# Second attention of a two-block kernel: products of split operands, remainders on GpSimd, out-projection by halves of k

## The reference

```python
def attn_mixer(h_ctx, h_lat, qkv_w, q_norm_w, k_norm_w, out_w, cos, sin, ctx_out):
    def project(u):                              # qkv_w: 1024 x 1536
        q, k, v = jnp.split(u @ qkv_w, [D_ATTN, D_ATTN + N_KV_HEADS * HEAD_DIM], axis=-1)
        q = rmsnorm(q.reshape(b, L, N_KV_HEADS, Q_PER_KV, HEAD_DIM), q_norm_w)
        k = rmsnorm(k.reshape(b, L, N_KV_HEADS, HEAD_DIM), k_norm_w)
        return q, k, v.reshape(b, L, N_KV_HEADS, HEAD_DIM)
    ...                                          # rope on q and k of the tokens
    s = jnp.einsum('bqkgd,bskd->bkgqs', q_blk, k) * scale      # keys: tokens and context
    p = jax.nn.softmax(s, axis=-1)
    o = jnp.einsum('bkgqs,bskd->bqkgd', p, v)
    out_lat = o.reshape(b, S, D_ATTN) @ out_w    # out_w: 1024 x 1024
# around it, in layer 1:
h_lat = rmsnorm(x, norm1_w[i]) * (1.0 + sc1l) + sh1l           # and h_ctx from ctx
x = x + g1l * o_lat
x = x + g2l * moe_ec(rmsnorm(x, norm2_w[i]) * (1.0 + sc2l) + sh2l, ...)
```

## Time and profile before

| | |
|---|---|
| median of three runs | 2139.0 us |
| profiled execution | 2138.3 us, its span 2136.4 us |
| TensorE matmul, busy share of the span | 93% |
| DVE, ACT, POOL, busy share | 44%, 31%, 5% |
| HBM read | 620.8 MB, 291 GB/s over the span |
| mean granted clock of TensorE | 0.984 |

### The profile page before, as it was taken

How to read it: one execution, slowest core, us unless ns; L and a number is a source line. 1 busy time by engine, 2 the same in 40 slices (tenths; PEclk the granted TensorE clock), 3 DMA queues, 4 the chain that set the end, 5 groups by cost and what they waited for, 6 DMA issues and landing times.

```text
span 2136.4 us, 24699 instructions
## 1 busy us (share of the span) xinstructions
PE 1988.2 (93%) x10028; PEld 1075.2 (50%) x10028; DVE 934.0 (44%) x1680; ACT 666.9 (31%) x1304; POOL 96.3 (5%) x105
## 2 busy tenths in 40 slices
PE   9988988999899999999899999988999899999887
PEld 6845644444578888878533333322444433333222
DVE  5667425454887888853612222221665301111101
ACT  5254313111577776752311110100244111111001
POOL 0101000000101000100000000000210000000000
PEclk9989989999999999999999999999999999999999
DMA  9637878998043334325599999999820699999997
GB/s 370 217 123 276 288 286 324 383 404 327 25 141 119 106 112 154 105 77 216 212 422 429 427 427 428 427 427 424 332 97 1 269 416 426 427 427 427 427 426 324
DMA packets 143376, 623.58 MB, mean 292 GB/s; under 512 B 10976, under 2 KB 61280, under 8 KB 105376
## 3 DMA queue, kind: packets, MB, share of 16 engines
q1 hardware_dynamic: 141104, 618.83, 72.7%
q10 hardware_dynamic: 2160, 3.18, 0.4%
HBM read 620.80 MB, written 1.18 MB: 291 GB/s over the span
## 4 chain that ended last, share of the span: by engine, by line
PE 73%; DMA 14%; DVE 7%; ACT 3%; issue 2%; SPq 1%; POOL 1%; DVEq 0%; POOLq 0%; ACTq 0%
PE bank L3216 21%; DMA slots<-in_moe_w 10%; PE bank L564 7%; PE bank L566 7%; PE bank L565 7%; PE bank L634 6%; PE bank L1972 4%; PE bank L3237 2%; DMA spare_slot<-in_moe_w 2%; PE bank L1999 2%; DMA hT<-in_moe_w 2%; PE bank L3187 2%; PE bank L2514 1%; PE bank L1102 1%; PE bank L1956 1%
## 5 line engine op out<-in xcount | busy, mean ns | idle before, releaser
L3216 PE MATMUL bank<-slots,xgTe 128*64 128x512 f32 (+1 forms) x1392 | 312.2, 594 | 28.5 <-DMA slots<-in_moe_w 28.5
L3486 DVE TENSOR_TENSOR actse<-sge,bank 32x512 f32<-32x512 f32 (+1 forms) x48 | 32.8, 683 | 501.9 <-PE bank L3216 273.5
L3216 PEld LDWEIGHTS bank<-slots,xgTe 128*64 128x64 f32 (+1 forms) x1392 | 93.5, 125 | 228.4 <-issue 193.8
L3379 ACT ACTIVATE sge<-bank 32x512 f32<-32x512 f32 (+1 forms) x48 | 28.4, 591 | 463.4 <-PE bank L3216 463.2
L3216 PE MATMUL bank<-slots,aTe 128*64 128x512 f32 (+1 forms) x688 | 156.9, 601 | 13.7 <-issue 12.5
L565 PE MATMUL bank<-slots_r 128*128 128x512 f32 x416 | 163.4, 393 | 0.0
L564 PE MATMUL bank<-hT_r,slots_r 128*128 128x512 f32 x384 | 155.6, 405 | 0.0
L566 PE MATMUL bank<-slots_r 128*128 128x512 f32 x384 | 152.0, 396 | 0.0
L3391 ACT ACTIVATE aTe<-bank 128x512 f32<-128x512 f32 x32 | 19.1, 597 | 282.9 <-PE bank L3290 282.9
L2419 DVE TENSOR_TENSOR slots_r<-slots,slots_r 128x2048 fp32r<-128x2048 f32 x32 | 76.7, 2396 | 68.2 <-ACT slots_r L2414 68.1
L3216 PEld LDWEIGHTS bank<-slots,aTe 128*64 128x64 f32 (+1 forms) x688 | 49.8, 126 | 105.6 <-issue 102.9
(11 more groups left out here) (615 smaller groups left out, 3320.8 us busy)
## 6 DMA issues: line engine op xcount, KB each, us to landing
slots<-in_moe_w SPq DMA_DIRECT2D x127, 2048.0 KB, 26.8
spare_slot<-in_moe_w SPq DMA_DIRECT2D x22, 2048.0 KB, 25.8
slots<-in_ada_w SPq DMA_DIRECT2D x20, 2048.0 KB, 10.9
extra0e<-in_moe_w SPq DMA_DIRECT2D x20, 2048.0 KB, 28.3
slots<-in_ssd_in_w SPq DMA_DIRECT2D x48, 512.0 KB, 5.3
slots<-in_moe_w_gate SPq DMA_DIRECT2D x20, 1024.0 KB, 9.0
slots<-in_moe_w_up SPq DMA_DIRECT2D x20, 1024.0 KB, 11.2
slots<-in_moe_w_down SPq DMA_DIRECT2D x19, 1024.0 KB, 15.1
```

Source lines behind the costliest of these rows:

```text
L3216: i = pe.matmul(bank[64 * n:64 * n + NJ * CAP, :], lhsT(4 * h + k), wv[:, 0, n * 512:(n + 1) * 512], start=(h == 0 and k == 0), stop=(h == ...
```

## The change

The eight products take three passes of split operands. ACT rounds each weight piece in two halves into a second slot ("qkv_high", slots 3, 1, 2); GpSimd subtracts and writes the remainder over the raw piece, in two halves of 128 x 2048. ACT rounds hT chunk by chunk into `h_high5`, which lies over `xn5`; DVE subtracts and writes the remainder over hT itself. The evictions are written out in a new order so that these steps come between them. The work is queued on each engine so: ACT rounds piece 0, squares, rounds piece 1, evicts and rounds; GpSimd makes the two remainders of piece 0, then the four roots, then the two of piece 1, and the two of piece 2 between the first query roots. The out-projection runs over the first four k of all four banks, then over the last four, and its first weight piece is free after the first half. Its two pieces lie in slots 0 and 6, the order of the ten places of the second expert stage is another, and the place `extra0` is free when the attention's last value product is done instead of at its last addition.

```diff
         for n in (0, 1, 2):
             weights(("qkv", n), [(0, KD, 512, rows("attn_qkv_w_2")[:, :, n * 512:(n + 1) * 512])], (6, 5, 4)[n])
+            ring.add(("qkv_high", n), (3, 1, 2)[n], 0)
         for n in range(2):
-            weights(("attn_out", n), [...], (3, 0)[n])
+            weights(("attn_out", n), [...], (0, 6)[n])
...
-        moe2_weights(1, (1, 2, 6, 5, SLOTS + 2, 4, 3, 0, SLOTS + 1, SLOTS + 3))
+        moe2_weights(1, (3, 5, 1, 4, SLOTS + 2, 2, SLOTS + 1, 0, 6, SLOTS + 3))
...
-                extra_room[l].freed = (ssd_added, TT) if l == 0 else att_added[-1]
+                extra_room[l].freed = (ssd_added, TT) if l == 0 else (bank_full, banks["att5", "pv", QH // 2 - 1].full)
...
+            h_high = nc.alloc_sbuf_tensor_at("h_high5", [P, KD, 2 * S], F32R, offset=shared_at)
+            h_low = hT_r
...
             def _(pe):
+                def product(tag, n, at, steps):
+                    b = banks.open(tag, ACTE)
+                    pe.wait_ge(*b.emptied)
+                    for k in range(KD):
+                        if steps is not None:
+                            pe.wait_ge(h5_split, steps + k)
+                        c = slice(at, at + P)
+                        i = matmul_split(pe, b.ap[:, :], (h_high[:, k, c], h_low[:, k, c]),
+                                         (rounded_qkv(n)[:, k, :], rounded_qkv(n, True)[:, k, :]), k == 0, k == KD - 1)
+                    i.then_inc(bank_full, 1)
+                    QKV[n][0].freed = QKV[n][1].freed = (bank_full, b.full)
...
                 for n in range(2):
-                    ...
-                        b, _ = gemm(pe, ("q5", n, t), lambda k: hT[:, k, S + t * P:S + (t + 1) * P], KD, t,
-                                    lambda k: wv[:, k, :], 512, ACTE)
+                    pe.wait_ge(w5_split, 2 * n + 2)
+                        product(("q5", n, t), n, S + t * P, 1 if (n, t) == (0, 0) else None)
+                pe.wait_ge(w5_split, 6)
                 for t in range(TT):
-                    b, _ = gemm(pe, ("kv5", t), lambda k: hT[:, k, t * P:(t + 1) * P], KD, t, lambda k: wv[:, k, :], 512, ACTE)
+                    product(("kv5", t), 2, t * P, KD + 1 if t == 0 else None)
...
-                for t in range(NT):
-                    for n in range(2):
-                        b, _ = gemm(pe, ("ao5", t, n), lambda k: oT[:, k, t * P:(t + 1) * P], KD, t, ...)
+                outs = [(t, n, banks.open(("ao5", t, n), DVE)) for t in range(NT) for n in range(2)]
+                for h in range(2):
+                    ...
+                    for t, n, b in outs:
+                        for k in range(4):
+                            i = pe.matmul(b.ap[:, :], oT[:, 4 * h + k, t * P:(t + 1) * P], wv[:, k, n * 512:(n + 1) * 512],
+                                          start=(h == 0 and k == 0), stop=(h == 1 and k == 3), skip_group_check=True)
+                    ...
             @block.gpsimd
             def _(pool):
+                def lower_w(n, j):
+                    pool.wait_ge(w5_rounded, 2 * n + j + 1)
+                    c = slice(4 * j, 4 * j + 4)
+                    pool.tensor_tensor(rounded_qkv(n, True)[:, c, :], raw_qkv(n)[:, c, :],
+                                       rounded_qkv(n)[:, c, :].bitcast(F32), ALU.subtract).then_inc(w5_split, 1)
+                lower_w(0, 0)
+                lower_w(0, 1)
                 norm.pool(pool)
-                qn.pool(pool)
+                lower_w(1, 0)
+                lower_w(1, 1)
+                qn.pool(pool, 0, 1)
+                lower_w(2, 0)
+                qn.pool(pool, 1, 2)
+                lower_w(2, 1)
+                qn.pool(pool, 2, len(QU))
                 kn.pool(pool)
...
             def _(act):
+                def round_w(n):
+                    raw, high = QKV[n]
+                    act.wait_ge(raw.sem, raw.full)
+                    act.wait_ge(*high.before.freed)
+                    for j in range(2):
+                        c = slice(4 * j, 4 * j + 4)
+                        act.activation(rounded_qkv(n)[:, c, :], raw_qkv(n)[:, c, :], ACT.Copy).then_inc(w5_rounded, 1)
+                def round_h(k, s_):
+                    b = banks["n5", k]
+                    act.wait_ge(emptied[b.by], b.done)
+                    c = slice((1 - s_) * S, (2 - s_) * S)
+                    act.activation(h_high[:, k, c], hT[:, k, c], ACT.Copy).then_inc(h5_rounded, 1)
+                round_w(0)
                 norm.scalar_squares(act, added)
-                norm.evacuate(act, ACTE)
+                round_w(1)
+                act.wait_ge(bank_full, banks["n5", KD - 1].full)
+                evict_h(act, ACTE, 1)
+                round_h(0, 0)
+                for k in range(3, KD, 2):
+                    evict_h(act, ACTE, k)
+                    round_h(k - 2, 0)
+                    round_h(k - 1, 0)
+                round_h(KD - 1, 0)
                 for n in range(2):
                     copy_out(act, ACTE, ("g15", 0, n), g1[:, n * 512:(n + 1) * 512], 512)
+                for k in range(KD):
+                    round_h(k, 1)
                 for n in range(2):
                     for t in range(NT):
                         copy_out(act, ACTE, ("q5", n, t), q[:, t, n * 512:(n + 1) * 512], 512)
+                        if (n, t) == (0, 0):
+                            round_w(2)
...
             def _(dve):
+                def lower_h(k, s_):
+                    dve.wait_ge(h5_rounded, KD * s_ + k + 1)
+                    c = slice((1 - s_) * S, (2 - s_) * S)
+                    dve.tensor_tensor(h_low[:, k, c], hT[:, k, c], h_high[:, k, c].bitcast(F32),
+                                      ALU.subtract).then_inc(h5_split, 1)
                 norm.vector_scale(dve)
-                norm.evacuate(dve, DVE)
+                for k in range(0, KD, 2):
+                    evict_h(dve, DVE, k)
+                    if k >= 4:
+                        lower_h(k - 4, 0)
+                        lower_h(k - 3, 0)
+                for k in range(KD - 4, KD):
+                    lower_h(k, 0)
+                for k in range(KD):
+                    lower_h(k, 1)
```

More of the change, by code:

```diff
@@ L372, in build @@
             weights(("qkv", n), [(0, KD, 512, rows("attn_qkv_w_2")[:, :, n * 512:(n + 1) * 512])], (6, 5, 4)[n])
+            ring.add(("qkv_high", n), (3, 1, 2)[n], 0)
         for n in range(2):
-            weights(("attn_out", n), [(0, 4, D, rows("attn_out_w_2")[:, 4 * n:4 * n + 4, :])], (3, 0)[n])
+            weights(("attn_out", n), [(0, 4, D, rows("attn_out_w_2")[:, 4 * n:4 * n + 4, :])], (0, 6)[n])
         queries_room = Piece(None, None, 0, None)
         ring.last[SLOTS + 2] = queries_room
-        moe2_weights(1, (1, 2, 6, 5, SLOTS + 2, 4, 3, 0, SLOTS + 1, SLOTS + 3))
+        moe2_weights(1, (3, 5, 1, 4, SLOTS + 2, 2, SLOTS + 1, 0, 6, SLOTS + 3))
         issued = [0]
@@ L716, in columns, with pool @@
                 return slice(self.at + u * self.H, self.at + (u + 1) * self.H)
-            def pool(self, pool):
-                for u in range(self.units):
+            def pool(self, pool, first=0, upto=None):
+                for u in range(first, self.units if upto is None else upto):
                     pool.wait_ge(heads_summed, self.before + u + 1)
@@ L3111, in expert_choice @@
                     piece.freed = (half_used, 3 * e + j // 2 + 1) if j % 2 == 0 else ((h1_full, h3_full, y_full)[j // 2], e + 1)
-                    if l == 0 and n % 8 == 7 or l == 1 and n % 10 == 8:
+                    if l == 0 and n % 8 == 7 or l == 1 and n % 10 == 6:
                         piece.ap = extra[0][:, :]
@@ L3555, in build @@
         with ExitStack() as scope:
+            shared_at = (nc.sbuf_base + 31) // 32 * 32
             shared = sb("xn5", [P, 4, D], scope=scope)
+            h_high = nc.alloc_sbuf_tensor_at("h_high5", [P, KD, 2 * S], F32R, offset=shared_at)
+            h_low = hT_r
+            h5_rounded, h5_split, w5_rounded, w5_split = (sem(x) for x in ("h5_rounded", "h5_split", "w5_rounded", "w5_split"))
+            QKV = [(ring["qkv", n], ring["qkv_high", n]) for n in range(3)]
             kk = sb("k5", [P, TT, KVH * 64], scope=scope)
@@ L3585, in build @@
             sin2 = const("sin2d").rearrange("p (t d) -> p t d", t=NT)
-            q_ready, k_ready = sem("q5_ready"), sem("k5_ready")
+            q_ready, k_ready, half_out = sem("q5_ready"), sem("k5_ready"), sem("half_out")
             to_qT = Transpose("qT5", lambda n, t: q[:, t, n * P:(n + 1) * P], QH // 2, P, lambda g, m: qT[:, g:g + m, :])
@@ L3591, in build, with rounded_qkv, raw_qkv @@
             block = whole
+            def rounded_qkv(n, low=False):
+                return rounded_slot(QKV[n][0 if low else 1].slot).rearrange("p (k n) -> p k n", k=KD)
+            def raw_qkv(n):
+                return QKV[n][0].ap.rearrange("p (k n) -> p k n", k=KD)
             @block.tensor
             def _(pe):
+                def product(tag, n, at, steps):
```

(31 more changed lines are left out.)

11 lines of the change are left out of this document (1 added, 10 removed).

## The result

The changed kernel takes 2143.6 us (median of 11 runs, 2140.3 to 2146.6), the kernel before 2138.4 (11 runs beside it). The ratio is 1.0025, 95% interval 1.0017 to 1.0033. The forecast was 2144.0. The profiled execution of after took 2144.6 us, its span 2142.7; the span before was 2136.4.

The account below looks back on a forecast made before the run. The second expert stage's start, set by the attention ahead, was taken to bound the kernel. 10.3 us saved on TensorE, outweighed by POOL remainders and holds, left the stage 5.7 us later: 2138.3 + 5.7 = 2144.0, range 2133 to 2155.

Parts of the forecast that it names:

- the fourth scaling: DVE's last norm scaling, held by POOL's third remainder: ends at 1523.6 instead of 1512.01, 11.5 us late.
- remainder six: POOL's last weight remainder, 1550.9 to 1554.9; the key/value products wait for it.
- restart: Expert weight loads resume when the second expert stage uses its first piece; 1693.56 before, near 1699 forecast; carries to the end.
- Remainder five: POOL's remainder after unit 0's root, 1542.0 to 1546.0; holds unit 0's last multiply (0.69 us) until 1546.5.
- the mutual hold: Claim that POOL and DVE exclude each other for a whole instruction, so DVE work waits out each POOL remainder.
- W: Time of one POOL weight remainder of 128x2048: estimated 4.0 us, between 2.01 and 6.0, entering the sum five times.
- ACT's work from the first eviction to the query copy: Half evictions, 16 roundings at 0.42 us and two gate copies on ACT: 11.7 us, 1525.3 to 1537.0.
- four roots: POOL's norm roots, back to back: one of 0.8 us and three of 1.68 us, from 1513.2 to 1519.0.
- The cheap rival: POOL remainders near 2.0 us each: 2134 us, deciding for faster below about 2.7 us each; chance 0.16.
- margin of 0.2%: Difference in total time taken as indistinguishable from none: 4.3 us, 2134.7 to 2143.3.
- The rival's half form: Only scaling four escapes POOL's hold, ACT starts 4 us sooner, half taken back: 2142; chance 0.12 with its full form.
- The costs set at nothing: Out-projection's new order, its later second weight piece and the expert loads behind it: claimed to add no time.

Follow-up runs that it names:

- e2: Changed kernel with POOL computing only half of each weight remainder (128x1024 instead of 128x2048), TensorE using it for the other half too: 2134.9 us.
- e3: Changed kernel with the six weight remainders on VectorE in the same places of the order, POOL doing only roots: 2136.9 us.
- e4: Changed kernel with the weight remainders on VectorE, in the order in which they are needed: 2132.0 us, ratio 0.9977 to the kernel before.
- e6: Changed kernel with only POOL's order altered: norm's roots first, remainders after the scalings and the queries' lower parts, then the heads' roots: 2144.2 us.
- e7: e4 with the last two remainders, those of the key and value piece, given back to POOL between the roots: 2138.7 us.
- e1: Changed kernel with POOL waiting for all four VectorE scalings before it begins its third remainder: 2142.1 us.
- e5: Kernel before with only the out-projection over k in halves, its first weight slot freed after the first half: 2138.5 us against 2138.6.

## Why the prediction was right

**The path.** Every station of it is in the trace: squares from 1506.45 (forecast 1507, before 1504.70); the fourth scaling held, done at 1523.36 (1523.6); ACT's evictions from 1525.43 (1525.3); remainder six done at 1553.84 (1554.9); last product near 1576.6 (1577.5); restart at 1698.35 (1699). Remainder five held the rstd instruction and not the multiply behind it, at the same cost. The cause, POOL's length times its places on the path plus the mutual hold, is shown by e2 (the length), e3 and e4 (the engine), e6 and e7 (the hold, in whatever place).

**W was mis-sized, and other terms made up for it.** 4.66 us instead of 4.0, five times, is 3.3 us more. Against it stood: ACT's work from the first eviction to the query copy, 9.5 us (1525.43 to 1534.90) instead of 11.7, a rounding of 128x256 being 0.33 (eight in 2.60 us) and not 0.42; four roots in 4.5 us (1513.81 to 1518.34) instead of 5.8; the weight half a us sooner. The last key copy came 4.7 us later, where the forecast had 5.7 for the end of the stage. So the hit within 0.4 us is in part luck. The cheap rival's bound doesn't follow from the sum: W = 2.7 gives 2137.5, which is not clear of before, and to fall under 2134.7 W would have to be about 2.1. That margin of 0.2% was itself too wide, since the intervals of the runs reach 0.08 to 0.10% to either side. The Trainium skill's price for such an instruction (GPSIMD Engine Reference, section 3.1: 4497 ns) agrees with the trace: 4503 to 4562 ns for the first three, up to 4967 for the others, beside which VectorE did more (that this is the reason is not shown).

**The rule behind the hold is narrower than I had it.** I wrote that POOL and DVE exclude each other for a whole instruction. Evictions out of PSUM are not held: six take 2.80 us beside a remainder (1523.93 in after, 1519.44 in e1) and 2.80 in e4, where POOL has nothing to do then (1516.91). The Trainium skill says this (SBUF — State Buffer, Who interferes with whom): the shared port pair is taken by a VectorE instruction in a two-port mode or with two SBUF inputs, not by one with at most one SBUF input outside those modes. The traces agree: the lower parts, with two SBUF inputs, are held, the evictions are not. The scaling and rstd have one SBUF input and were held; no row names their mode. The rival's half form (only scaling four wins, half given back to a held eviction, 2142) has e1's time, 2142.1, by chance: in e1 the evictions ran, the lower parts were held, and by the last key copy all of the 4 us was given back.

**The last 1.5 us.** The profiled span is 6.3 us longer, the restart only 4.8 later. The rest is the first expert's third product, here at the lower clock (granted 0.51 from 1713.1 to 1716.5; in before 1.00 from 1708.3 to 1710.0). Its first half, after, then before:

```profile
1713.06 3.54 PE L3217 MATMUL bank<-queries_slot,aTe 128*32 128x512 f32 x8 [0.73 <-issue]
```
```profile
1708.27 1.91 PE L3216 MATMUL bank<-queries_slot,aTe 128*32 128x512 f32 x8 [0.73 <-issue]
```

Both halves together take 5.6 us in four of the nine profiles (after, e2, e5, e6) and 3.8 in the other five. From the restart to the end of the span it is 444.4 to 444.7 us in those four and 442.5 to 442.8 in those five. The gather ahead of the expert takes 5.47 us in five profiles and 3.84 in four. Neither follows the kernel in a way that I can see: such 1.6 to 1.8 us come and go with the execution, and a difference of that size can't be read from one profile. What decides it stays open.

**The costs set at nothing** held: the out-projection in halves moves no time (e5). The new order of the ten expert places and the earlier release of `extra0` were not run alone; but the distance from the last key tile to the restart is 117.7 us in after and before alike, and the stretch from the restart to the end has the same two lengths with the old order (before 442.8, e5 444.6) as with the new one.

## What to carry to other kernels

Work moved to GpSimd is not moved off VectorE if both operands lie in SBUF: here it takes twice as long there (4.5 against 2.25 us for 128x2048) and holds the next VectorE instruction between SBUF operands to its end (evictions out of PSUM ran on), so the cheaper place was VectorE itself, in the order in which the results are needed: with that, e4, the split products pay (2132.0). Where a race between two such instructions is lost, winning it may only move the hold to the next VectorE instruction between SBUF operands, as in e1; count the holds, not the races. A trade that makes a hot loop shorter must be added up from the first instruction that its operands need: here 10.2 us of TensorE were bought with 11.8 us ahead of it and a wait behind.

## What was not expected of the hardware

The length of a held VectorE instruction followed POOL's instruction and not its own size: rstd with eight columns goes from 0.17 to 4.47 us beside a remainder of 128x2048 and to 2.25 beside one of half the size (e2), a scaling of 1024 columns from 0.75 to 4.99 and 2.83. And the hold goes both ways: a POOL instruction of one column takes 2.45 us behind a VectorE remainder (e4).
